# Modulation sums moved from VectorE to ScalarE (scaling) and GpSimd (adding) in a three-layer forward pass

## The chip, the cores and the metric

The kernel runs on one core of one Trainium2 chip. The metric is the device time of one execution in microseconds (us). The engines are TensorE (PE, with its weight loads as PEld), VectorE (DVE), ScalarE (ACT), GpSimd (POOL) and SyncE (SP, which only issues transfers here). Each engine takes its instructions in the order of the program and waits on semaphores for the others.

## The reference

One token sequence of 256 positions and 2048 features goes through three layers: a hybrid of gated linear attention and sparse attention with a feed-forward part, an attention layer with context tokens (`ev`), and a pooling layer (`od`). Everything is fp32. What the change touches is the modulation of the second and third layer, a vector times matrix product per layer:

```python
def _modulation(cvec, w, b):
    m = jax.nn.silu(cvec) @ w + b          # w: 2048 x 6144
    m = m[..., None, :]
    return m[..., :D_MODEL], m[..., D_MODEL:2 * D_MODEL], m[..., 2 * D_MODEL:]

# attention layer: for the tokens and for the context
shift, scale, gate = _modulation(c, mod_w, mod_b)
shift_c, scale_c, gate_c = _modulation(c_ctx, mod_w, mod_b)
h = _rmsnorm(x, pre_g) * (1 + scale) + shift
# pooling layer: for the tokens alone
shift, scale, gate = _modulation(c, mod_w, mod_b)
```

The rest is matrix products of 256 tokens with weights of 2048 or more rows, norms, and attention.

## The kernel before

The main work is a stream of 305 steps. A step makes one tile of 128 output features for 256 tokens: it takes two halves of 1024 x 128 weights (`w_main`, 512 KB each). Each half lands in one of four buffers `raw`; ScalarE copies it to `w_hi` in the rounded type fp32r (L776, function `hi`), VectorE subtracts to get the rest `w_lo` (L1002, function `lo`), and TensorE multiplies three products per 128x128 block: hi x hi, hi x lo, lo x hi (L411 to L413). That is 48 matmuls in a step, two PSUM banks in turn. The steps are grouped in stages (`STAGES`): conv, rest, out, up0, down0, up1, down1, up2, down2, ev_kv, ev_q, ev_z, ev_out, od_u, pool, od_z, od_out. In down2 a step has 36 matmuls; in out, down2, ev_out and od_out TensorE adds one matmul a step for a sum of squares, whose square ScalarE makes (L785).

Beside the main stream runs a side stream. Twelve of the stages (`MOD_GROUPS`) carry, in their first 16 steps, one group of modulation weights: 16 side tiles of 128 rows x 1024 columns (`w_side`, 512 KB), one a step, in two buffers `side`. VectorE multiplies the tile by the 128 values of silu(c) that belong to its rows and adds it to the running sum `mod_sum` (L1014, function `add_mod`). In four stages (`BOTH`: groups 0 to 3, which are rest, out, up0 and down0) it does so a second time from the same tile for the context vector, into the second half of `mod_sum`. When the sixteenth tile is in, TensorE sums `mod_sum` over the partitions with 128x1 matmuls at the end of the stage (L468, function `sum_mods`), VectorE reads them (L1038) and clears `mod_sum` (L1019).

The order of the work is written out by hand: each engine has its own program, with loops of two steps (`steps`). In step k of a stage
- SP (`loads`) issues the two raw loads of step k+2, each when `w_lo` of the half two steps before is done (`lo_ready`), and then side tile k, when tile k-2 has been added (`mods_added`);
- ScalarE (`ahead`) makes `w_hi` of step k+1, when the raw halves have landed and TensorE has used the same buffers for step k-1 (`halves_used`), and then what the stage asks for: a Silu (L754 in the up stages, L763 in the z stages, L838 in rest) or a square (L785);
- VectorE (`reading`) makes `w_lo` of step k+1, then the mod sum of tile k, then waits for TensorE to finish step k and reads its result out of PSUM (in conv with four taps, L1124 and L1127; in the up and z stages with a gate and a split, L1402 to L1408).

Of the kernel before, what the change touches and what calls it, by code (L numbers as in the profile page):

```python
# [25 lines left out]
ACT = mybir.ActivationFunctionType  # L26
# [119 lines left out]
def build(nc, x, ctx_in, w_main, w_side, cols_in, cons_in, gla_masks_in, counts_in, gate_w2_in, cmp_w2_in, out):  # L146
    stack = ExitStack()
    with stack:
# [3 lines left out]
        def S(name):  # L152
            if name not in sems:
                sems[name] = stack.enter_context(nc.semaphore(name))
            return sems[name]
# [135 lines left out]
        lo_ready = S("lo_ready")  # L291
        halves_used = S("halves_used")
        mods_added = S("mods_added")
        mods_summed = S("mods_summed")
        cmp_used = S("cmp_used")
        dve_read = S("dve_read")
# [105 lines left out]
        def _(pe):  # L402
# [58 lines left out]
            def sum_mods(stage):  # L461

                g = MOD_STAGES.index(stage)
                pe.wait_ge(mods_added, DT * (g + 1))
                vecs = 2 if MOD_GROUPS[stage] in BOTH else 1
                for t in range(8):
                    for c in range(vecs):
                        mm = pe.matmul(ps[:, 7, vecs * t + c:vecs * t + c + 1], mod_sum[:, c, t * P:(t + 1) * P],  # L468
                                       ones[:, 0:1], start=True, stop=True)
                mm.then_inc(mods_summed, 1)  # L470
# [275 lines left out]
        def gate_silu_steps(act, stage, silus):  # L746

            def extra(i, k):
                if k % 2:
                    return  # L750
                s = FIRST[stage] + k
                act.wait_ge(halves_used, i * 4 + (2 * s + 2))
                act.wait_ge(S("gate_y"), i + (silus + 1))
                act.activation(sg[:, 0, :], ps[:, s % 2, 0:T], ACT.Silu).then_inc(silu_ready, 1)  # L754
            return extra

# [11 lines left out]
        def _(act):  # L768
            def hi(i, s):

                for c in range(2):
                    slot = 2 * (s % 2) + c
                    act.wait_ge(raw_full[slot], i * 16 + 16 * (s // 2 + 1))
                    if s >= 2:
                        act.wait_ge(halves_used, i * 4 + (2 * s + c - 3))
                    act.activation(w_hi[:, slot, :], raw[:, slot, :], ACT.Copy).then_inc(hi_ready, 1)  # L776

            def ahead(stage, first=0, extra=None, squared=None, of=None):

                base = dve_reads(stage)  # L780

                def square(i, k):
                    act.wait_ge(dve_read, i * 2 + (base + k + 1))
                    src = of[:, k:k + 1, :] if isinstance(i, int) else of[:, bass.ds(i * 2 + k, 1), :]
                    act.activation(sq_tile[:, k % 2:k % 2 + 1, :], src, ACT.Square).then_inc(S(f"{squared}_sq"), 1)  # L785

                def body(i, k):
                    if FIRST[stage] + k + 1 < STEPS:
                        hi(i, FIRST[stage] + k + 1)
                    if extra is not None:  # L790
                        extra(i, k)
                    if squared is not None and k:
                        square(i, k - 1)
                if squared is not None:
                    first = 2
                steps(act, stage, body, first=first, last=2 if stage == "od_out" else 0)
                if squared is not None:
                    square(0, COUNT[stage] - 1)

# [6 lines left out]
            def root(name, buf):  # L806
                act.wait_ge(S(f"{name}_rs"), 1)
                act.activation(buf, buf, ACT.Sqrt).then_inc(S(f"{name}_rs"), 1)
# [10 lines left out]
            def from_psum(name, dst):  # L819
# [8 lines left out]
            hi(0, 0)  # L828
            act.activation(csil[:, :, :], col("cvec", 0, 32).rearrange("p (t c) -> p t c", c=2), ACT.Silu)\
               .then_inc(S("csil"), 1)  # L830
            root("attn", rstd[:, :])
            shift_hi("attn", sq, a_hi, None)
            ahead("conv", first=2)

            def conv_silu(i, k):

                if k % 2 == 0 and k < 28:
                    act.activation(pr[:, bass.ds(i, 1), :], pr[:, bass.ds(i, 1), :], ACT.Silu)  # L838
            act.wait_ge(dve_read, 16)
            ahead("rest", extra=conv_silu)  # L840
            act.activation(pr[:, 14:16, :], pr[:, 14:16, :], ACT.Silu).then_inc(S("g_silu"), 1)
# [150 lines left out]
                act.activation(o_tok[:, 0, g * 512:(g + 1) * 512], ps[:, g, :], ACT.Copy).then_inc(S("o_tok0"), 1)  # L992


        @block.vector
        def _(dve):
            def lo(i, s):
# [6 lines left out]

            def add_mod(stage, i, k):

                n, m = mod_half(stage, k)
                vecs = 2 if MOD_GROUPS[stage] in BOTH else 1
                dve.wait_ge(side_full[n % 2], i * 16 + 16 * (n // 2 + 1))
                if k or not isinstance(i, int):  # L1010
                    dve.wait_ge(mods_added, i * 2 + m)
                for c in range(vecs):
                    value = csil[:, k:k + 1, c] if isinstance(i, int) else csil[:, bass.ds(i * 2 + k, 1), c]
                    ins = dve.scalar_tensor_tensor(out=mod_sum[:, c, :], in0=side[:, n % 2, :], scalar=value,  # L1014
                                                   in1=mod_sum[:, c, :], op0=ALU.mult, op1=ALU.add)
                ins.then_inc(mods_added, 1)

            def clear_mods(g):
                dve.memset(mod_sum[:, :, :], 0.0).then_inc(S("mods_clear"), 1)  # L1019
# [632 lines left out]
```

## Time and profile before

| | |
|---|---|
| median of 3 runs | 2452.38 us (2448.59 to 2456.3) |
| span of the profiled execution | 2443.0 us |
| its own time against that median | 9.4 us lie around the span |
| TensorE busy, mean granted clock | 2199.2 us (90%), 0.920 |
| VectorE busy | 1576.2 us (65%) |
| ScalarE busy | 995.4 us (41%) |
| GpSimd busy | 0.2 us (4 small memsets) |
| transfers | 433.76 MB, mean 178 GB/s |

The profile gives the span, from the first to the last instruction, of one execution; the time of that execution outside the span is not recorded, so the difference to the median stands for it. Busy shares are averages over stages with different limits. The stages stand in the trace at these times: conv 42 to 149 us, rest to 323, the attention work of the first layer to 549, out to 657, up0 687 to 870, down0 to 974, up1 to 1161, down1 to 1255, up2 to 1395, down2 to 1488, ev_kv 1534 to 1616, ev_q to 1711, attention to 1872, ev_z to 1957, ev_out to 2059, and then the stages of the pooling layer, which carry no side tiles.

### The profile page before, as it was taken

The numbers are of one execution on the slowest core, as the hardware profiler recorded it, in microseconds if no ns is written. First come the engines' busy times: TensorE is split into PE (matmuls) and PEld (weight loads), VectorE is DVE, ScalarE is ACT, GpSimd is POOL, SyncE is SP. The second block draws the span as 40 slices with busy tenths as digits, with TensorE's granted clock in tenths as the row PEclk, the third lists the DMA queues.
The fourth block names the chain that finished last, engine by engine and source line by source line (L and its number), as shares of the span: only waits on it lengthen the run. The fifth ranks groups of instructions, "written<-read, shape, count | busy, mean of one in ns | idle before, by whom it ended". The sixth has DMA issues, their size and how long they took to land.

```text
span 2443.0 us, 45011 instructions
## 1 busy us (share of the span) xinstructions
PE 2199.2 (90%) x16718; PEld 2127.6 (87%) x16718; DVE 1576.2 (65%) x2077; ACT 995.4 (41%) x1230; POOL 0.2 (0%) x4
## 2 busy tenths in 40 slices
PE   5999987489799999999999996999689998888997
PEld 5999986369799999999999985999378998888997
DVE  5888564548787577764767576346656766666544
ACT  4346631333355632343333344223245633424642
POOL 0000000000000000000000000000000000000000
PEclk8999966569899999999999997999699998998998
DMA  4767521007567586765878682357003875444552
GB/s 174 245 239 270 184 80 44 0 1 241 172 220 236 174 287 227 263 226 186 269 259 273 200 294 85 100 181 273 6 1 127 271 248 171 138 138 142 185 181 95
DMA packets 119530, 433.76 MB, mean 178 GB/s; under 512 B 13216, under 2 KB 13600, under 8 KB 119216
## 3 DMA queue, kind: packets, MB, share of 16 engines
q1 hardware_dynamic: 119472, 432.98, 53.2%
q8 instruction: 37, 0.61, 0.1%
q14 instruction: 21, 0.17, 0.0%
HBM read 430.83 MB, written 2.10 MB: 177 GB/s over the span
## 4 chain that ended last, share of the span: by engine, by line
PE 69%; DVE 16%; DMA 8%; issue 4%; ACT 2%; SPq 1%; DVEq 1%; ACTq 0%
PE ps L411 19%; PE ps L413 19%; PE ps L412 19%; DMA side<-w_side 8%; DVE w_lo L1002 3%; PE ps L643 2%; PE ps L473 2%; PE ps L468 1%; DVE sq L1064 1%; PE ps L480 1%; DVE mod_sum L1014 1%; DVE at_max L1339 1%; PE ps L512 1%; PE ps L437 1%; PE ps L632 1%
## 5 line engine op out<-in xcount | busy, mean ns | idle before, releaser
L411 PE MATMUL ps<-a_hi,w_hi 128*128 128x256 f32 x3280 | 939.8, 287 | 58.4 <-DVE w_lo L1002 33.4
L412 PE MATMUL ps<-a_lo,w_hi 128*128 128x256 f32 x3280 | 934.2, 285 | 0.0
L413 PE MATMUL ps<-a_hi,w_lo 128*128 128x256 f32 x3280 | 933.8, 285 | 0.0
L776 ACT ACTIVATE w_hi<-raw 128x1024 fp32r<-128x1024 f32 x610 | 634.2, 1056 | 699.3 <-PE ps L413 636.0
L1002 DVE TENSOR_TENSOR w_lo<-raw,w_hi 128x1024 fp32r<-128x1024 f32 x610 | 718.8, 1220 | 108.3 <-ACT w_hi L776 105.6
L411 PEld LDWEIGHTS ps<-a_hi,w_hi 128*128 128x128 f32 x3280 | 635.8, 194 | 66.1 <-DVE w_lo L1002 35.5
L412 PEld LDWEIGHTS ps<-a_lo,w_hi 128*128 128x128 f32 x3280 | 636.0, 194 | 0.0
L413 PEld LDWEIGHTS ps<-a_hi,w_lo 128*128 128x128 f32 x3280 | 635.8, 194 | 0.0
L411 PE MATMUL ps<-b_hi,w_hi 128*128 128x256 f32 x1664 | 485.0, 291 | 17.6 <-DVE w_lo L1002 8.4
L413 PE MATMUL ps<-b_hi,w_lo 128*128 128x256 f32 x1664 | 473.8, 285 | 0.0
L412 PE MATMUL ps<-b_lo,w_hi 128*128 128x256 f32 x1664 | 473.7, 285 | 0.0
L1014 DVE SCALAR_TENSOR_TENSOR mod_sum<-side,csil,mod_sum 128x1024 f32<-128x1024 f32 x256 | 323.0, 1282 | 153.8 <-DMA side<-w_side 153.4
L411 PEld LDWEIGHTS ps<-b_hi,w_hi 128*128 128x128 f32 x1664 | 322.4, 194 | 24.2 <-issue 10.5
L412 PEld LDWEIGHTS ps<-b_lo,w_hi 128*128 128x128 f32 x1664 | 322.4, 194 | 1.2
L413 PEld LDWEIGHTS ps<-b_hi,w_lo 128*128 128x128 f32 x1664 | 322.2, 194 | 0.0
L1137 DVE COPY pr<-ps 128x256 f32 (+1 forms) x93 | 39.4, 424 | 171.4 <-PE ps L413 171.4
L754 ACT ACTIVATE sg<-ps 128x256 f32<-128x256 f32 x44 | 16.9, 385 | 146.8 <-PE ps L413 146.7
L632 PE MATMUL ps<-pr 128*128 128x256 f32 (+1 forms) x192 | 52.7, 422 | 18.0 <-DVE pr L1462 6.3
L776 ACT ACT_TABLE_LOAD x46 | 59.0, 1283 | 17.4 <-DVE pr L1127 11.3
L632 PEld LDWEIGHTS ps<-pr 128*128 128x128 f32 x192 | 37.4, 221 | 32.8 <-DVE pr L1462 7.2
L1371 DVE COPY pr<-ps 128x128 f32<-128x128 f32 x48 | 14.0, 292 | 62.5 <-PE ps L643 32.7
L473 PE MATMUL ps<-cons,prob 128*128 128x128 f32 x176 | 34.1, 327 | 20.5 <-DVE prob L1366 12.8
(242 smaller groups left out, 1462.6 us busy)
## 6 DMA issues: line engine op xcount, KB each, us to landing
raw<-w_main SPq DMA_DIRECT2D x610, 512.0 KB, 4.3
side<-w_side SPq DMA_DIRECT2D x200, 512.0 KB, 5.6
x_tok<-x_in SPq DMA_DIRECT2D x4, 512.0 KB, 6.0
ctx_tok<-ctx_tok SPq DMA_DIRECT2D x1, 2048.0 KB, 9.2
y_out<-o_tok SPq DMA_DIRECT2D x4, 512.0 KB, 2.7
cons<-cons_in SPq DMA_DIRECT2D x1, 542.0 KB, 8.0
table<-counts_tab SPq DMA_DIRECT2D x1, 512.0 KB, 10.1
table<-masks_in SPq DMA_DIRECT2D x1, 448.0 KB, 11.1
```

The source lines that it names most:

```text
L411: pe.matmul(out_ap, wh, act_hi[:, kt, :], start=first and n == 0, stop=False)
L412: pe.matmul(out_ap, wh, act_lo[:, kt, :], start=False, stop=False)
L413: mm = pe.matmul(out_ap, wl, act_hi[:, kt, :], start=False, stop=last and n == len(blocks) - 1)
L437: return pe.matmul(ps[:, 2, 0:T], ones, sq_tile[:, k % 2, :], start=k == 0, stop=k == COUNT[stage] - 1)
L468: mm = pe.matmul(ps[:, 7, vecs * t + c:vecs * t + c + 1], mod_sum[:, c, t * P:(t + 1) * P], ones[:, 0:1], start=True, stop=True)
L473: return pe.transpose(ps[0:ncols, bank, at_col:at_col + rows], src_ap, ident[base:base + rows, base:base + rows])
L632: mm = pe.matmul(ps[:, 2 + h % 3, part * T:part * T + a["keys"]], pr[:, a["q"](h), a["cols"]], pr[:, a["k"](h, part), 0:a["keys"]], start= ...
L643: mm = pe.matmul(ps[:, 5 + h % 2, 0:P], a["v"](h, part, b), a["prob_t"][:, h % 2, n, :], start=n == 0, stop=a["kind"] != "n" and n == len( ...
L776: act.activation(w_hi[:, slot, :], raw[:, slot, :], ACT.Copy).then_inc(hi_ready, 1)
L1002: dve.tensor_tensor(w_lo[:, slot, :], raw[:, slot, :], w_hi[:, slot, :].bitcast(F32), ALU.subtract)\
L1014: ins = dve.scalar_tensor_tensor(out=mod_sum[:, c, :], in0=side[:, n % 2, :], scalar=value, in1=mod_sum[:, c, :], op0=ALU.mult, op1=ALU.add)
L1137: dve.tensor_copy(tile(dst, i, k + k0), psum_tile(bank)).then_inc(dve_read, 1)
```

## The change

The running sum for the token vector leaves VectorE. ScalarE multiplies the side tile in place by the silu(c) values of its rows (`scale_mod`, a Copy with a scale that is a pointer to 128 values), and GpSimd, which had no program, adds the scaled tile to `mod_sum` (`add`). A side buffer is free when GpSimd has added it. In the four stages of `BOTH`, VectorE still makes the sum for the context vector from the unscaled tile, and ScalarE may overwrite the tile only after that (`mods_ctx`). ScalarE's loops are now cut after 16 steps in the stages with side tiles, and two indices are adapted to that.

```diff
@@ TensorE, sum_mods
                 pe.wait_ge(mods_added, DT * (g + 1))
+                pe.wait_ge(mods_ctx, DT * sum(MOD_GROUPS[name] in BOTH for name in MOD_STAGES[:g + 1])) \
+                    if any(MOD_GROUPS[name] in BOTH for name in MOD_STAGES[:g + 1]) else None
@@ ScalarE, gate_silu_steps
-                act.wait_ge(S("gate_y"), i + (silus + 1))
+                act.wait_ge(S("gate_y"), i + (silus + k // 2 + 1))
@@ ScalarE, ahead
+                def scale_mod(i, k):
+                    n, m = mod_half(stage, k)
+                    act.wait_ge(side_full[n % 2], i * 16 + 16 * (n // 2 + 1))
+                    if MOD_GROUPS[stage] in BOTH:
+                        g = MOD_STAGES.index(stage)
+                        both = DT * sum(MOD_GROUPS[name] in BOTH for name in MOD_STAGES[:g]) + k
+                        act.wait_ge(mods_ctx, i * 2 + (both + 1))
+                    value = csil[:, k:k + 1, 0] if isinstance(i, int) else csil[:, bass.ds(i * 2 + k, 1), 0]
+                    act.activation(side[:, n % 2, :], side[:, n % 2, :], ACT.Copy, scale=value).then_inc(mods_scaled, 1)
+
                 def body(i, k):
                     if FIRST[stage] + k + 1 < STEPS:
                         hi(i, FIRST[stage] + k + 1)
+                    if stage in MOD_GROUPS and k < DT:
+                        scale_mod(i, k)
                     if extra is not None:
                         extra(i, k)
...
-                steps(act, stage, body, first=first, last=2 if stage == "od_out" else 0)
+                steps(act, stage, body, first=first, last=2 if stage == "od_out" else 0,
+                      splits=[DT] if stage in MOD_GROUPS else ())
@@ GpSimd, a program of its own
+        @block.gpsimd
+        def _(pool):
+            def add(i, m, k):
+                n = m + (2 * CMP_HALVES if m >= CMP_AT else 0)
+                pool.wait_ge(mods_scaled, i * 2 + (m + 1))
+                if m or not isinstance(i, int):
+                    pool.wait_ge(mods_added, i * 2 + m)
+                pool.tensor_tensor(mod_sum[:, 0, :], side[:, n % 2, :], mod_sum[:, 0, :], ALU.add).then_inc(mods_added, 1)
+
+            for g in range(len(MOD_STAGES)):
+                pool.wait_ge(S("mods_clear"), g + 1)
+                add(0, DT * g, 0)
+                add(0, DT * g + 1, 1)
+                with pool.Fori(0, DT // 2 - 1) as i:
+                    add(i, DT * g + 2, 2)
+                    add(i, DT * g + 3, 3)
@@ VectorE, add_mod
+                if MOD_GROUPS[stage] not in BOTH:
+                    return
                 n, m = mod_half(stage, k)
-                vecs = 2 if MOD_GROUPS[stage] in BOTH else 1
+                g = MOD_STAGES.index(stage)
+                both = DT * sum(MOD_GROUPS[name] in BOTH for name in MOD_STAGES[:g]) + k
                 dve.wait_ge(side_full[n % 2], i * 16 + 16 * (n // 2 + 1))
-                if k or not isinstance(i, int):
-                    dve.wait_ge(mods_added, i * 2 + m)
-                for c in range(vecs):
-                    value = csil[:, k:k + 1, c] if isinstance(i, int) else csil[:, bass.ds(i * 2 + k, 1), c]
-                    ins = dve.scalar_tensor_tensor(out=mod_sum[:, c, :], in0=side[:, n % 2, :], scalar=value,
-                                                   in1=mod_sum[:, c, :], op0=ALU.mult, op1=ALU.add)
-                ins.then_inc(mods_added, 1)
+                if both or not isinstance(i, int):
+                    dve.wait_ge(mods_ctx, i * 2 + both)
+                value = csil[:, k:k + 1, 1] if isinstance(i, int) else csil[:, bass.ds(i * 2 + k, 1), 1]
+                dve.scalar_tensor_tensor(out=mod_sum[:, 1, :], in0=side[:, n % 2, :], scalar=value,
+                                         in1=mod_sum[:, 1, :], op0=ALU.mult, op1=ALU.add).then_inc(mods_ctx, 1)
```

Where it moves instructions can be seen in the loops of two steps. On ScalarE, the loop of stage up0 (steps 0 to 15 of it now, all 32 before) stood so before:

```order
L775 ISA [waits raw_full0]
L776 ACT_TABLE_LOAD
L776 ACTIVATE w_hi<-raw 128x1024 [waits halves_used]
L775 REGISTER_ALU [waits raw_full1]
L776 ACTIVATE w_hi<-raw 128x1024 [waits halves_used]
L753 REGISTER_ALU [waits halves_used]
L754 ACT_TABLE_LOAD
L754 ACTIVATE sg<-ps 128x256 [waits gate_y]
L775 REGISTER_ALU [waits raw_full2]
L776 ACTIVATE w_hi<-raw 128x1024 [waits halves_used]
L776 ACTIVATE w_hi<-raw 128x1024 [waits halves_used,raw_full3]
```

and stands so now (all but the register rows; L780 is the old L776, L758 the old L754):

```order
L780 ACT_TABLE_LOAD
L780 ACTIVATE w_hi<-raw 128x1024 [waits halves_used]
L780 ACTIVATE w_hi<-raw 128x1024 [waits halves_used]
L797 ISA [waits side_full0]
L799 ISA [waits mods_ctx]
L799 ACTIVATE side<-side,csil 128x1024
L758 ACT_TABLE_LOAD
L758 ACTIVATE sg<-ps 128x256 [waits gate_y]
L780 ACTIVATE w_hi<-raw 128x1024 [waits halves_used]
L780 ACTIVATE w_hi<-raw 128x1024 [waits halves_used,raw_full3]
L799 ISA [waits mods_ctx]
L799 ACTIVATE side<-side,csil 128x1024
```

A scaling with its waits for the side tile and for VectorE's context sum has come in behind each pair of `w_hi`; the two table loads stay.

On VectorE, one step in the loop of stage down0 (both vectors) stood so before:

```order
L1011 ISA [waits side_full0]
L1014 ISA [waits mods_added]
L1014 SCALAR_TENSOR_TENSOR mod_sum<-side,csil,mod_sum 128x1024
L1014 ISA
L1014 SCALAR_TENSOR_TENSOR mod_sum<-side,csil,mod_sum 128x1024
L1389 ISA [waits halves_used]
L1389 TENSOR_TENSOR res<-ps,res 128x256
L1002 TENSOR_TENSOR w_lo<-raw,w_hi 128x1024 [waits hi_ready]
L1002 TENSOR_TENSOR w_lo<-raw,w_hi 128x1024 [waits hi_ready]
```

and stands so now (L1038 is the old L1002, L1426 the old L1389):

```order
L1050 ISA [waits side_full0]
L1052 ISA [waits mods_ctx]
L1052 SCALAR_TENSOR_TENSOR mod_sum<-side,csil,mod_sum 128x1024
L1426 ISA [waits halves_used]
L1426 TENSOR_TENSOR res<-ps,res 128x256
L1038 TENSOR_TENSOR w_lo<-raw,w_hi 128x1024 [waits hi_ready]
L1038 TENSOR_TENSOR w_lo<-raw,w_hi 128x1024 [waits hi_ready]
L1050 REGISTER_ALU [waits side_full1]
```

One of two sums is gone, and the next sum stands behind the next two `w_lo` as before. GpSimd's loop is two adds with a wait for the scaling and for the add before.

## Rows read from the trace of the kernel before

**Rows 1.** The page's head and part 1: busy us (share) xinstructions.

```profile
span 2443.0 us, 45011 instructions
PE 2199.2 (90%) x16718; PEld 2127.6 (87%) x16718; DVE 1576.2 (65%) x2077; ACT 995.4 (41%) x1230; POOL 0.2 (0%) x4
```

**Rows 2.** Busy us by window: conv, rest, out, up0, down0, up1, down1, down2, ev_z, ev_out.

```profile
core 0: us, PE busy (x) PEld busy (x) DVE busy (x) ACT busy (x) POOL busy (x), PEclk, DMA share, GB/s
42.00:149.00 107.00, 99.57 (x782) 97.18 (x782) 88.25 (x115) 32.85 (x31) 0.00 (x0) 0.96 0.74 250
149.00:245.00 96.00, 96.00 (x782) 96.00 (x783) 82.80 (x81) 60.31 (x60) 0.00 (x0) 0.97 0.75 255
549.00:651.00 102.00, 100.95 (x800) 99.75 (x801) 83.39 (x81) 37.26 (x47) 0.00 (x0) 0.98 0.75 245
687.00:780.00 93.00, 87.19 (x716) 85.91 (x715) 77.59 (x84) 50.05 (x51) 0.00 (x0) 1.00 0.74 244
872.00:967.00 95.00, 92.50 (x761) 92.29 (x760) 81.99 (x81) 33.92 (x32) 0.00 (x0) 0.99 0.80 268
975.00:1160.00 185.00, 185.00 (x1539) 185.00 (x1537) 113.38 (x128) 70.07 (x80) 0.00 (x0) 1.00 0.67 222
1163.00:1254.00 91.00, 91.00 (x762) 91.00 (x760) 63.93 (x65) 33.62 (x32) 0.00 (x0) 1.00 0.81 270
1397.00:1485.00 88.00, 79.61 (x595) 73.36 (x594) 62.43 (x65) 38.92 (x47) 0.00 (x0) 0.98 0.84 280
1872.00:1954.00 82.00, 79.87 (x666) 79.58 (x664) 65.39 (x86) 51.90 (x58) 0.00 (x0) 1.00 0.82 272
1958.00:2058.00 100.00, 99.25 (x797) 98.02 (x796) 64.33 (x65) 38.20 (x47) 0.00 (x0) 0.99 0.73 247
```

**Rows 3.** Waits: engine line waited for: total us, times, longest.

```profile
DVE mod_sum L1014 <- DMA side<-w_side: 153.4, 145, 3.4
```

**Rows 4.** The chain that ended last, in conv: start us, us, what.

```profile
105.97 6.07 DMA side<-w_side
```

**Rows 5.** Timeline of VectorE in conv, from one late side tile on.

```profile
99.24 1.28 DVE L1014 SCALAR_TENSOR_TENSOR mod_sum<-side,csil,mod_sum 128x1024 f32<-128x1024 f32 x1 [0.99 <-DMA side<-w_side]
100.44 0.48 DVE L1124 TENSOR_SCALAR pr<-ps,cols 128x256 f32 x1
...
102.82 2.35 DVE L1002 TENSOR_TENSOR w_lo<-raw,w_hi 128x1024 fp32r<-128x1024 f32 x2
...
112.29 1.29 DVE L1014 SCALAR_TENSOR_TENSOR mod_sum<-side,csil,mod_sum 128x1024 f32<-128x1024 f32 x1 [1.18 <-DMA side<-w_side]
```

**Rows 6.** Part 5, costliest groups: xcount | busy us, mean ns | idle before.

```profile
L776 ACT ACTIVATE w_hi<-raw 128x1024 fp32r<-128x1024 f32 x610 | 634.2, 1056 | 699.3 <-PE ps L413 636.0
L1002 DVE TENSOR_TENSOR w_lo<-raw,w_hi 128x1024 fp32r<-128x1024 f32 x610 | 718.8, 1220 | 108.3 <-ACT w_hi L776 105.6
L1014 DVE SCALAR_TENSOR_TENSOR mod_sum<-side,csil,mod_sum 128x1024 f32<-128x1024 f32 x256 | 323.0, 1282 | 153.8 <-DMA side<-w_side 153.4
L754 ACT ACTIVATE sg<-ps 128x256 f32<-128x256 f32 x44 | 16.9, 385 | 146.8 <-PE ps L413 146.7
L776 ACT ACT_TABLE_LOAD x46 | 59.0, 1283 | 17.4 <-DVE pr L1127 11.3
```

**Rows 7.** The chain in the first attention: reciprocal over 1024, tensor-tensor over 2048 elements.

```profile
420.78 6.56 DVE g_rs L1249
...
430.63 2.30 DVE g_y L1258
```

**Rows 8.** The chain in down2: a landing.

```profile
1420.98 5.17 DMA side<-w_side
```

**Rows 9.** Timeline of TensorE at the ends of conv, down0 and ev_z.

```profile
145.37 0.80 PE L468 MATMUL ps<-cons,mod_sum 128*128 128x1 f32 x3 [3.39 <-DVE mod_sum L1014]
...
966.34 0.81 PE L468 MATMUL ps<-cons,mod_sum 128*128 128x1 f32 x4 [2.50 <-DVE mod_sum L1014]
...
1954.00 0.72 PE L468 MATMUL ps<-cons,mod_sum 128*128 128x1 f32 x5 [2.13 <-DVE mod_sum L1014]
```

More of the change, by code:

```diff
@@ L293, in build @@
         mods_added = S("mods_added")
+        mods_ctx = S("mods_ctx")
+        mods_scaled = S("mods_scaled")
         mods_summed = S("mods_summed")
@@ L830, in _ @@
                .then_inc(S("csil"), 1)
+            act.wait_ge(S("csil"), 1)
             root("attn", rstd[:, :])
@@ L837, in conv_silu @@
                 if k % 2 == 0 and k < 28:
-                    act.activation(pr[:, bass.ds(i, 1), :], pr[:, bass.ds(i, 1), :], ACT.Silu)
+                    at = bass.ds(i + k // 2, 1)
+                    act.activation(pr[:, at, :], pr[:, at, :], ACT.Silu)
             act.wait_ge(dve_read, 16)
```

## Prediction, before the result was known

> **What bounds the kernel now.** I read the page's busy shares first: TensorE is busy 90% of the span, VectorE 65%, ScalarE 41%, GpSimd not at all [rows 1]. VectorE is thus not a bound by its total, and taking work off it pays only where TensorE waits for it. So the windows by stage come next [rows 2]. From the matmul counts a step (48 matmuls, 49 with the sum of squares, 36 in down2) takes 91/762 x 48 = 5.73 us where TensorE is the limit (down1, and 185/1539 x 48 = 5.77 in up1, whose pattern up2 and ev_q repeat). For two steps, the natural unit because `side` has two buffers: conv 107/782 x 96 = 13.1 us, rest 11.8, out 12.5 (a step has 49), up0 12.5, down0 12.0, down1 11.5, ev_z 11.8, ev_out 12.3 with its 49. Only conv, up0, down2, slightly down0 and ev_z run behind TensorE's pace; there the excess over 11.5 us is all that a relief of VectorE can return.
>
> The waits tell what it is: VectorE stood 153 us, 145 times, for side transfers [rows 3]. The chain shows the loop in conv [rows 4, 5]: transfer lands, mod sum (1.20 us to the next start), conv taps (2.38), two `w_lo` (2.36), 0.79 until SP has issued two raw loads and the next side load, 6.07 us until that has landed, 0.25 until the sum starts: 13.05 us for two steps. SP is in order, so the side load stands behind raw loads that wait for `lo_ready`. That is the loop the change rewires.
>
> **The change part by part.** Durations [rows 6]: `w_hi` 1.06, `w_lo` 1.22, one mod sum 1.28, ScalarE's table load 1.28, a small Silu over 256 elements 0.39, which I take for the square and the residual add of that size too (0.4).
>
> VectorE loses 192 of 256 mod sums (192 x 1.28 = 246 us busy). ScalarE gains 192 scalings of 1024 elements per partition; the trace has no scaling with a pointer, the nearest row is `w_hi`, same engine and shape, so 1.06 each, 204 us on an engine that was 59% idle. That total costs nothing by itself. GpSimd gains 192 adds of 128x1024. No row shows such an add: the cheapest end is VectorE's `w_lo`, same operation and shape, 1.22; the dear end is the slowest instruction over 1024 elements in the trace, the reciprocal at 6.56 us. The add is nearer the first; I take 2.30, the row of a VectorE tensor-tensor over twice the elements [rows 7], because an engine that the kernel never uses for arithmetic should not be counted as fast as VectorE. The Trainium skill (GPSIMD Engine Reference, Performance versus the Vector engine) measured 4497 ns for an add over 2048 fp32 elements; an estimate by halving is 2.25 us. No run here shows it yet, and the sum would be the same by it.
>
> What matters is the new order of waits. A scaling waits for the side transfer, and behind it in ScalarE's queue stands the `w_hi` of the next step but one, and so `w_lo`, the raw loads and the next side load.
>
> (a) Stages with one vector, adds not in the way. Loop for two steps: scale 1.06, two `w_hi` 2.12, second `w_lo` 1.22, issue 0.79, landing. Landings on the chain are 5.17 to 6.07 [rows 4, 8]; I take 5.5 where loads are evenly spaced, 6.3 with the start in conv. Conv: 11.5, under the 11.8 of its neighbour, so 1.3 x 8 = 11 us gained. down1, up1, up2, ev_q: 10.7 to 11.1 (0.39 for the Silu), under TensorE's 11.5: no change. down2, the one stage where transfers and not TensorE set the pace before and after: scale 1.06 + square 0.4 + 2.12 + 1.22 = 4.80 stand in the place of sum 1.28 + residual add 0.4 + two `w_lo` 2.36 = 4.04: +0.76 x 8 = 6. ev_z: 1.06 + table 1.28 + 0.39 + 2.12 + 1.22 + 0.79 + 5.5 = 12.4 against 11.8: +0.54 x 8 = 4.
>
> (b) Stages with both vectors (rest, out, up0, down0). VectorE's sum must read `side` before ScalarE overwrites it, and VectorE's next sum stands behind the `w_lo` of the next step. That closes a loop within one step: sum 1.28, scale 1.06, [table load and Silu], two `w_hi` 2.12, second `w_lo` 1.22, next sum. Down0 and out: 5.68 and 6.1 (square), just under their 6.0 and 6.25: 0. In rest and up0 each pair holds two table loads and one Silu (the order shows them): 2 x (1.28 + 1.06 + 1.28 + 2.12 + 1.22) + 0.39 = 14.3. Rest: 14.3 - 11.8 = 2.5 x 8 = +20. Up0: 14.3 - 12.5 = 1.8 x 8 = +15. Before, the table loads were covered because `w_hi` came 1.5 steps ahead of its use; behind the scaling this lead is gone.
>
> (c) Ends. TensorE's 128x1 matmuls need the last sum. It comes later by scale + add (+3.36), less the sum 1.28 it replaces, some 0.2 for a hand-over: 2.3. In conv, down0 and ev_z TensorE already waited there (3.39, 2.50, 2.13 [rows 9]): 7. In out, down1, down2, ev_q and ev_out the margin hides between 0 and all of it: I take 1 each, 5. In rest and the up stages the sum is ready long before. Together +12.
>
> (d) Whether the add and VectorE's instructions run side by side. The trace has no GpSimd work, so: cheap end 0, dear end that an add and an instruction of VectorE with two SBUF operands (`w_lo`, sum) exclude each other for the add's whole 2.30. The add starts with the first `w_hi` after the scaling, so `w_lo`, due 1.06 later, would wait till 2.30. Then in (b) the step is 1.28 + 1.06 + 2.30 + 1.22 + 1.22 = 7.08: down0 +1.09 x 16 = 17, out +0.83 x 16 = 13; rest and up0 nothing, since table load and `w_hi` last 2.34. In (a) the loop is 1.06 + 2.30 + 2.44 + 0.79 + 5.5 = 12.1: down1, up1, up2, ev_q +0.63 x 8 x 4 = 20; conv 5.80 in place of 5.94: -1 instead of -11; down2 5.80 - 4.04 = 1.76 x 8 = 14 instead of 6; ev_out under its 12.3: 0. I take the dear end: in loops without slack each overlap shows in full, and the two would contend for 2.30 + 2.44 of every 5.8 us. The Trainium skill (SBUF — State Buffer, Who interferes with whom) says that a VectorE instruction with two SBUF inputs and a GpSimd instruction that reads SBUF exclude each other, whoever comes second blocked for the whole instruction. It speaks against this change; no run here shows it yet. By it the sum is the dear one, without it the cheap one.
>
> Sum, dear end: 20 + 15 + 13 + 17 + 20 + 14 + 4 - 1 + 12 = +114 us. Cheap end: 20 + 15 + 6 + 4 - 11 + 12 = +46. The profiled span is 2443.0 [rows 1]; the median of the runs is 2452.4, so 9.4 us lie around it, and 2443 + 114 + 9.4 = 2567.
>
> **The rivals.**
> Side by side (the cheap end): GpSimd slows nobody. For it: nothing in the trace couples the two. Against it: nothing in the trace could. 2443 + 46 + 9 = 2498.
> GpSimd becomes the bound: an add of 6.56. SP may load `side` again only after the add; from 2.12 + 1.22 + 0.79 = 4.1 us on the add outlasts that path and decides. Two steps are then 1.06 + 6.56 + 0.79 + 5.5 = 13.9 (15.2 with both vectors): down1, up1, up2, ev_q, ev_z, ev_out +2.4, 2.4, 2.4, 2.4, 2.1, 1.6 x 8 = 106; rest, out, up0, down0 +3.4, 2.7, 2.7, 3.2 x 8 = 96; down2 and conv +36; ends +50: about 2740. Against it: 6.56 is a reciprocal's.
> Not slower: VectorE, free of the 153 us of waits, delivers `w_lo` early, and ScalarE's waits for the side transfer fall into the 636 us that `w_hi` waits for TensorE anyway [rows 6]. This decides if the loop of (b) stays under 5.73 us a step in rest and up0, i.e. if sum and scaling overlap the `w_hi` of another step. Then conv -11, up0 -1.0 x 8, down0 -0.5 x 8, ev_z -0.3 x 8: -25, or 2427; with the 12 of the ends 2440. Against it: ScalarE's queue is in order and the scaling stands in front.
>
> **Numbers.** Exclusion 0.50 (2567), side by side 0.28 (2498), not slower 0.11 (2427 to 2450), GpSimd the bound 0.07 (over 2650), else 0.04. What can be told from no change here is 0.3%, 7 us. The forecast's own range is 2530 to 2610 (landing 5.2 to 6.1 us: 40 pairs x 0.9); with side by side it reaches down to 2480, and up to 2640 for an add of 3 us. Faster 0.08, same 0.05, slower 0.87.
>
> **What would show it.** Rest and up0 at about 14.3 us for two steps, VectorE's `w_lo` waiting for ScalarE's `w_hi`, and `w_hi` ending waits on `side`: (b). Down0 and out at 7.1 a step, with long `w_lo` or `w_lo` starting when an add ends: exclusion; at 6.0 and 6.25 and `w_lo` still 1.22: side by side. Conv at 11.8: (a) without exclusion. Adds over 4 us with SP's side loads released by GpSimd: the third case. Rest and up0 still under 12.5 would prove (b) wrong.

## The result, and the profile after

The changed kernel takes 2582.96 us in the median of 4 runs (2579.88 to 2586.41), the kernel before 2454.34 us (2448.59 to 2464.99): 5.4% slower, ratio 1.0536 with a 95% interval of 1.05 to 1.0573. The forecast was 2567 us.

The page's head, part 1 and four groups of part 5 of the changed kernel, in the place of [rows 1, 6] (L1038 is `w_lo`, L780 `w_hi`, L799 the scaling, L1021 the add, L1052 the context sum):

```profile
span 2584.6 us, 45692 instructions
PE 2247.6 (87%) x16718; PEld 2157.3 (83%) x16718; DVE 1517.5 (59%) x1885; ACT 1147.8 (44%) x1394; POOL 464.5 (18%) x196
L1038 DVE TENSOR_TENSOR w_lo<-raw,w_hi 128x1024 fp32r<-128x1024 f32 x610 | 877.1, 1478 | 336.9 <-ACT w_hi L780 334.4
L1021 POOL TENSOR_TENSOR mod_sum<-side,mod_sum 128x1024 f32<-128x1024 f32 x192 | 464.3, 2418 | 1732.0 <-ACT side L799 1710.5
L799 ACT ACTIVATE side<-side,csil 128x1024 f32<-128x1024 f32 x192 | 221.0, 1151 | 578.7 <-DMA side<-w_side 351.9
L1052 DVE SCALAR_TENSOR_TENSOR mod_sum<-side,csil,mod_sum 128x1024 f32<-128x1024 f32 x64 | 81.6, 1275 | 0.0
```

VectorE made 192 instructions fewer, yet its busy time fell by only 59 us and not by 246. Most of the rest is in its 610 `w_lo`, untouched by the change, which went from 1220 to 1478 ns in the mean: 158 us. The 141 of them that ran beside an add of GpSimd took 2.34 us in the mean, the 455 that met no add 1.22. The add takes 2.42 us (taken: 2.30), the scaling 1.15 (taken: 1.06). The waits, in the place of [rows 3] (total us, times, longest):

```profile
ACT side L799 <- DMA side<-w_side: 351.9, 125, 7.4
DVE w_lo L1038 <- ACT w_hi L780: 334.4, 167, 5.2
ACT w_hi L780 <- PE ps L415: 287.0, 153, 6.9
ACT side L799 <- DVE mod_sum L1052: 226.9, 64, 8.6
PE ps L413 <- DVE w_lo L1038: 96.0, 65, 17.0
```

VectorE's wait for side transfers has become ScalarE's, and `w_lo` now waits 334 us for `w_hi` (106 before [rows 6]): ScalarE's copies come late because the scaling stands in front of them.

By stage: the time from one clear of `mod_sum` to the next (L1019, now L1056) read from both profiled executions; gains and losses in us.

| stretch ending with | before | after | difference | forecast, with its end |
|---|---|---|---|---|
| conv | 107.1 | 105.9 | -1.3 | +1.3 |
| rest | 173.3 | 195.1 | +21.8 | +20 |
| out (with the attention work of layer 1) | 334.4 | 361.9 | +27.5 | +14 |
| up0 | 213.4 | 229.7 | +16.3 | +15 |
| down0 | 103.0 | 125.5 | +22.5 | +19 |
| up1, up2 | 327.8 | 336.3 | +8.5 | +10 |
| down1 | 93.9 | 102.8 | +8.8 | +6 |
| down2 | 93.1 | 101.8 | +8.7 | +15 |
| ev_q (with norms, ev_kv) | 222.2 | 232.0 | +9.7 | +6 |
| ev_z (with attention) | 245.8 | 261.5 | +15.7 | +6 |
| the rest of the program (ev_out) | 486.5 | 490.1 | +3.6 | +1 |

VectorE, ScalarE and GpSimd in one step of down0 (start us, us, engine, line, operation, idle before and its releaser; three views, one below the other):

```profile
993.26 3.74 DVE L1038 TENSOR_TENSOR w_lo<-raw,w_hi 128x1024 fp32r<-128x1024 f32 x2 [1.95 <-ACT w_hi L780]
996.92 1.27 DVE L1052 SCALAR_TENSOR_TENSOR mod_sum<-side,csil,mod_sum 128x1024 f32<-128x1024 f32 x1
1000.47 3.80 DVE L1038 TENSOR_TENSOR w_lo<-raw,w_hi 128x1024 fp32r<-128x1024 f32 x2 [1.94 <-ACT w_hi L780]
...
998.34 1.15 ACT L799 ACTIVATE side<-side,csil 128x1024 f32<-128x1024 f32 x1 [4.16 <-DVE mod_sum L1052]
999.39 1.99 ACT L780 ACTIVATE w_hi<-raw 128x1024 fp32r<-128x1024 f32 x2
...
999.65 2.40 POOL L1021 TENSOR_TENSOR mod_sum<-side,mod_sum 128x1024 f32<-128x1024 f32 x1 [4.87 <-ACT side L799]
```

The loop within one step can be read off: sum from 996.92, scaling from 998.34, `w_hi` from 999.39, the add from 999.65 to 1002.05; the two `w_lo` begin at 1000.47 but take 3.80 us in place of 2.36, because the first ends about 1 us after the add does. From one such pair to the next it is 7.21 us (1000.47 - 993.26); the forecast was 7.08. In up0 the table load replaces the exclusion:

```profile
778.66 1.28 DVE L1052 SCALAR_TENSOR_TENSOR mod_sum<-side,csil,mod_sum 128x1024 f32<-128x1024 f32 x1
783.65 2.36 DVE L1038 TENSOR_TENSOR w_lo<-raw,w_hi 128x1024 fp32r<-128x1024 f32 x2 [2.39 <-ACT w_hi L780]
...
780.10 1.16 ACT L799 ACTIVATE side<-side,csil 128x1024 f32<-128x1024 f32 x1 [2.80 <-DVE mod_sum L1052]
781.27 1.28 ACT L780 ACT_TABLE_LOAD   x1
782.56 2.00 ACT L780 ACTIVATE w_hi<-raw 128x1024 fp32r<-128x1024 f32 x2
...
781.33 2.41 POOL L1021 TENSOR_TENSOR mod_sum<-side,mod_sum 128x1024 f32<-128x1024 f32 x1 [5.06 <-ACT side L799]
```

Here the add is over (783.74) just when `w_lo` starts, which stays at 2.36 for two. Two steps take 14.8 us against a forecast of 14.3 (783.65 - 768.86, where the pair two steps earlier starts).

### The profile page after: what moved, and what is told of

The parts are those of the page before. It is cut to its first block, busy times and chain, and to the rows that moved or that the text cites. A ratio compares the mean times of both kernels' runs of the same rounds, so it can differ in the third digit from the quotient of the medians.

```text
span 2584.6 us, 45692 instructions
## 1 busy us (share of the span) xinstructions
PE 2247.6 (87%) x16718; PEld 2157.3 (83%) x16718; DVE 1517.5 (59%) x1885; ACT 1147.8 (44%) x1394; POOL 464.5 (18%) x196
## 4 chain that ended last, share of the span: by engine, by line
PE 47%; DVE 18%; DMA 13%; issue 12%; ACT 7%; SPq 1%; POOL 1%; ACTq 1%; DVEq 1%; POOLq 0%
DMA side<-w_side 13%; PE ps L413 12%; PE ps L415 12%; PE ps L414 12%; DVE w_lo L1038 5%; ACT w_hi L780 3%; PE ps L647 2%; DVE mod_sum L1052 2%; PE ps L477 2%; PE ps L472 2%; POOL mod_sum L1021 1%; PE ps L484 1%; DVE sq L1101 1%; SPq L348 1%; PE ps L636 1%
## 5 line engine op out<-in xcount | busy, mean ns | idle before, releaser
L1038 DVE TENSOR_TENSOR w_lo<-raw,w_hi 128x1024 fp32r<-128x1024 f32 x610 | 877.1, 1478 | 336.9 <-ACT w_hi L780 334.4
L1021 POOL TENSOR_TENSOR mod_sum<-side,mod_sum 128x1024 f32<-128x1024 f32 x192 | 464.3, 2418 | 1732.0 <-ACT side L799 1710.5
L780 ACT ACTIVATE w_hi<-raw 128x1024 fp32r<-128x1024 f32 x610 | 618.9, 1049 | 300.5 <-PE ps L415 287.0
L413 PE MATMUL ps<-b_hi,w_hi 128*128 128x256 f32 x1664 | 490.2, 295 | 31.5 <-DVE w_lo L1038 22.9
L799 ACT ACTIVATE side<-side,csil 128x1024 f32<-128x1024 f32 x192 | 221.0, 1151 | 578.7 <-DMA side<-w_side 351.9
L1052 DVE SCALAR_TENSOR_TENSOR mod_sum<-side,csil,mod_sum 128x1024 f32<-128x1024 f32 x64 | 81.6, 1275 | 0.0
L1439 DVE TENSOR_TENSOR gated<-pr,sg 128x256 f32<-128x256 f32 x32 | 32.5, 1015 | 62.3 <-ACT sg L767 62.3
L472 PEld LDWEIGHTS ps<-cons,mod_sum 128*128 128x128 f32 x256 | 42.2, 259 | 31.9 <-POOL mod_sum L1021 31.8
L472 PE MATMUL ps<-cons,mod_sum 128*128 128x1 f32 x256 | 42.6, 298 | 30.0 <-POOL mod_sum L1021 30.0
L636 PE MATMUL ps<-pr 128*128 128x256 f32 (+1 forms) x192 | 54.9, 438 | 15.7 <-DVE pr L1499 5.4
## 6 DMA issues: line engine op xcount, KB each, us to landing
table<-masks_in SPq DMA_DIRECT2D x1, 448.0 KB, 11.2
```

Of the source, the lines that this page charges most:

```text
L413: pe.matmul(out_ap, wh, act_hi[:, kt, :], start=first and n == 0, stop=False)
L636: mm = pe.matmul(ps[:, 2 + h % 3, part * T:part * T + a["keys"]], pr[:, a["q"](h), a["cols"]], pr[:, a["k"](h, part), 0:a["keys"]], start= ...
L799: act.activation(side[:, n % 2, :], side[:, n % 2, :], ACT.Copy, scale=value).then_inc(mods_scaled, 1)
L1021: pool.tensor_tensor(mod_sum[:, 0, :], side[:, n % 2, :], mod_sum[:, 0, :], ALU.add).then_inc(mods_added, 1)
L1038: dve.tensor_tensor(w_lo[:, slot, :], raw[:, slot, :], w_hi[:, slot, :].bitcast(F32), ALU.subtract)\
L1052: dve.scalar_tensor_tensor(out=mod_sum[:, 1, :], in0=side[:, n % 2, :], scalar=value, in1=mod_sum[:, 1, :], op0=ALU.mult, op1=ALU.add).the ...
```

## Experiments

All runs of a kernel stand beside runs of the kernel before on the same chip; the ratio is to those, with its 95% interval.

The forecast's word exclusion means here that an add of GpSimd and an instruction of VectorE with two SBUF operands can't run at the same time.

**Take the add's time away.** GpSimd adds 8 of 1024 columns.

```diff
-pool.tensor_tensor(mod_sum[:, 0, :], side[:, n % 2, :], mod_sum[:, 0, :], ALU.add).then_inc(mods_added, 1)
+pool.tensor_tensor(mod_sum[:, 0, 0:8], side[:, n % 2, 0:8], mod_sum[:, 0, 0:8], ALU.add).then_inc(mods_added, 1)
```

> The changed kernel with GpSimd adding 8 of the 1024 columns: the order and all hand-overs stay, the add's time goes (the sums of the other columns are left out). Theory 1 (exclusion: the add keeps VectorE's two-operand instructions waiting for its whole 2.4 us): back to the cheap end, about 2454 + 50 = 2504 us (2490 to 2520), w_lo at 1.22 instead of 1.48 us mean, down0 6.0 and out 6.25 us a step. Theory 2 (no exclusion, the price is in the hand-overs between three engines): only the ends get shorter by the add, 8 x 2.1 = 17 us, so about 2565, and down0 stays above 7 us a step.

Measured: 2506.55 us, ratio 1.0204 (1.0173 to 1.0235). `w_lo` is back at 1221 ns:

```profile
L1038 DVE TENSOR_TENSOR w_lo<-raw,w_hi 128x1024 fp32r<-128x1024 f32 x610 | 719.4, 1221 | 299.6 <-ACT w_hi L780 296.5 <-DVE mod_sum L1056 1.9 <-DVE pr L1560 0.2
```

down0 takes 109.8 us (125.5), down1 93.9 (as before the change), conv 98.8 (107.1 before: the relief of VectorE is real, and the only one). rest (194.3) and up0 (227.9) stay long. Theory 1 holds, at the forecast's cheap end of 2498 (+46) to within 9 us: the new order costs 50 us, and the other 1016 columns of the adds 76 more, part of which could be GpSimd's time alone; the next run looks at that. Two stages are dearer than the cheap end had them: down0 is 6.8 us above its time before the change where the sum had 2.3, and ev_z (256.7) is 10.9 above where it had 6.3.

**Keep GpSimd busy without reading.** The 8 columns, and then two fills.

```diff
+                pool.tensor_tensor(mod_sum[:, 0, 0:8], side[:, n % 2, 0:8], mod_sum[:, 0, 0:8], ALU.add)
+                pool.memset(mod_sum[:, 0, 8:HALF], 0.0)
+                pool.memset(spare[:, :], 0.0).then_inc(mods_added, 1)
```

> The changed kernel with GpSimd adding 8 columns and then filling 1016 + 512 columns with zeros (the sums are left out): GpSimd stays busy, an estimated 1.5 to 2.5 us per tile, but reads almost nothing. If VectorE waits only for GpSimd's reads: w_lo 1.22, time as in the run with 8 columns plus the ends, 2505 to 2525 us. If VectorE waits for whatever GpSimd does in SBUF: w_lo above 1.4 us mean and 2550 to 2585 us.

Measured: 2519.02 us, ratio 1.0259 (1.0223 to 1.0296). Its groups:

```profile
L1023 POOL MEMSET mod_sum<- 128x1016 f32 x192 | 181.6, 946 | 0.0
L1024 POOL MEMSET spare<- 128x512 f32 x192 | 100.9, 526 | 0.0
L1022 POOL TENSOR_TENSOR mod_sum<-side,mod_sum 128x8 f32<-128x8 f32 x192 | 44.4, 231 | 1819.1 <-ACT side L800 1805.2 <-DVE mod_sum L1059 13.9
L1041 DVE TENSOR_TENSOR w_lo<-raw,w_hi 128x1024 fp32r<-128x1024 f32 x610 | 719.4, 1221 | 299.0 <-ACT w_hi L781 295.9 <-DVE mod_sum L1059 1.9 <-DVE pr L1563 0.2
```

And its timeline in down0, GpSimd and VectorE:

```profile
987.19 0.20 POOL L1022 TENSOR_TENSOR mod_sum<-side,mod_sum 128x8 f32<-128x8 f32 x1 [4.87 <-ACT side L800]
987.33 0.94 POOL L1023 MEMSET mod_sum<- 128x1016 f32 x1
988.22 0.52 POOL L1024 MEMSET spare<- 128x512 f32 x1
...
988.09 2.36 DVE L1041 TENSOR_TENSOR w_lo<-raw,w_hi 128x1024 fp32r<-128x1024 f32 x2 [1.95 <-ACT w_hi L781]
```

The fills overlap the first `w_lo` (988.09 to 988.74) and it isn't stretched. Only 0.65 us overlap here, less than the add's, but in the whole trace 54 `w_lo` ran beside fills for 0.5 us or more, and all of them took 1.21 to 1.23 us. So VectorE's two-operand instruction waits for the add and not for the fill. The Trainium skill (SBUF — State Buffer, Who interferes with whom) says that a VectorE instruction with two SBUF inputs contends with a GpSimd instruction that reads SBUF and not with one that only writes it; this run and the one with full adds agree with it. By these runs alone it could be something else in which an add differs from a fill.

The fills did hold another instruction, the cast from SBUF to SBUF in the up and z stages, first VectorE and then GpSimd:

```profile
2002.15 0.29 DVE L1446 CAST b_hi<-gated 128x256 f32 x1
2005.76 1.06 DVE L1446 CAST b_hi<-gated 128x256 f32 x1 [0.15 <-DVE gated L1442]
...
2005.27 0.94 POOL L1023 MEMSET mod_sum<- 128x1016 f32 x1
2006.15 0.52 POOL L1024 MEMSET spare<- 128x512 f32 x1
```

The first cast meets no fill, the second ends 0.15 us after the second fill; 10 of the 76 casts took 0.77 to 1.45 us.

With this run the change can be split. The spans of the profiled executions, less the attention work of the first layer (whose length varies from kernel to kernel, see below), grow by 55 us from the kernel before to the 8-column adds, by 4 from there to the fills, and by 71 from the fills to the full adds. GpSimd's time as such is thus cheap (though the fills keep it busy for 1.7 us per tile, not 2.4), and the hold on VectorE is the dear part.

**The exclusion alone, in the old order.** The kernel before with an add per side tile on GpSimd that nobody waits for; it starts when VectorE's sum of that tile is done, and writes bf16.

```diff
+                pool.wait_ge(mods_added, i * 2 + (m + 1))
...
+                pool.tensor_tensor(spare[:, :], cons[:, 0:1024], cons[:, 128:1152], ALU.add).then_inc(spared, 1)
```

> The kernel before with one GpSimd add of 128x1024 per side tile beside it, started by each mod sum; it reads constants and writes a spare tile, and nobody waits for it. Exclusion: the next two w_lo wait for the add's end, 2.4 us after the sum instead of 0.4: +2 us in each loop of two steps that has no slack. With 1.28 + 2.4 + 2.36 + 0.79 + 5.8 = 12.6 against 11.5: +9 in down1, up1, up2, ev_q, ev_z each, +16 in down2, +14, 8, 8, 12 in rest, out, up0, down0, 0 in conv (its taps read PSUM): 2454 + 105, so 2540 to 2570 us, w_lo 1.4 to 1.6 us mean. No exclusion: 2454 and w_lo 1.22.

Measured: 2607.64 us, ratio 1.0647 (1.0622 to 1.0672), `w_lo` 1617 ns. The exclusion alone costs more than the whole change did, and 38 to 68 us more than I had reckoned (2540 to 2570). It is not the changed kernel's exclusion to the letter: here each add starts just when the next `w_lo` may. Its timeline in up1 shows two things that I left out, VectorE first, GpSimd below:

```profile
1111.05 4.56 DVE L1021 TENSOR_TENSOR w_lo<-raw,w_hi 128x1024 fp32r<-128x1024 f32 x2
1118.16 2.15 DVE L1425 CAST b_hi<-gated 128x256 f32 x1
...
1111.29 3.24 POOL L1004 TENSOR_TENSOR spare<-cons 128x1024 bf16<-128x1024 f32 x1 [4.48 <-DVE mod_sum L1033]
1117.77 2.39 POOL L1004 TENSOR_TENSOR spare<-cons 128x1024 bf16<-128x1024 f32 x1 [3.24 <-DVE mod_sum L1033]
```

An add that comes in while `w_lo` runs takes 3.24 us: it waits too, so whoever comes second waits. And the small cast of 256 columns, with one SBUF operand, took 2.15 us; the 39 of its 76 executions that met an add took 1.2 us or more, the other 37 0.30: not only two-operand instructions are held. up1 and up2 (201.8 and 154.2 us; 187.8 and 140.0 before), where that cast stands in the loop, lost 14 us each for the 9 I gave them. That is the smaller part of the miss: out itself lost 15 us (8 reckoned), up0 16 (8), down0 19 (12) and rest 19 (14), and 9 us lie in the attention work of the first layer, where no add runs. down2 lost 12.8 for 16.

**Undo one part.** The four stages with both vectors as before, the other eight changed (ScalarE's scaling and the adds skipped for `BOTH`, both sums on VectorE).

```diff
-                    if stage in MOD_GROUPS and k < DT:
+                    if stage in MOD_GROUPS and MOD_GROUPS[stage] not in BOTH and k < DT:
                         scale_mod(i, k)
...
+            alone = [g for g in range(len(MOD_STAGES)) if MOD_GROUPS[MOD_STAGES[g]] not in BOTH]
+            for j, g in enumerate(alone):
...
+                for c in range(2):
+                    value = csil[:, k:k + 1, c] if isinstance(i, int) else csil[:, bass.ds(i * 2 + k, 1), c]
```

> The change in the eight stages with one vector only; rest, out, up0 and down0 have both sums on VectorE again, as before. By the intervals between the clears of mod_sum, rest gained 22, out 27 (with the attention work), up0 16 and down0 22 us through the change: 87 in all. If each stage pays for its own order, the time is 2583 - 87 = 2496 us (2488 to 2506). If the price lies in the transfers or in GpSimd over the whole program, it stays above 2520.

Measured: 2528.5 us, ratio 1.0301 (1.0266 to 1.0336), so 32 us over what was expected. rest, up0 and down0 came back to 173.0, 216.1 and 105.7, and out itself to its 112.1 before the change. Two things had been reckoned wrongly. Part of the 27 us of the stretch that ends with out is not out's: 9 us of it are in the attention work here too (below). And the stages with one vector were longer than in the changed kernel's profile (down1 106.0 against 102.8, up2 148.9 against 144.4), 14 us together. That called for the control:

> The changed kernel as it is, beside the next three kernels on one chip: 2583 us within 0.3%, as before. If transfers land later here than in its first profile (side 5.6 us instead of 5.2 to 5.3 in down1 and down2), the stages with one vector take about 3 us more each, as they did in the run with both sums back on VectorE, and the time comes to about 2595; if not, that run's extra has another cause.

Measured: the changed kernel again, 2591.91 us, ratio 1.0573 (1.055 to 1.0597), with side transfers landing in 5.7 us in down1 (5.2 in its first profile), and down1 105.0, up2 148.1. That fits a landing in series with the loop, which no slack absorbs, in down1 and the up stages; ev_z (260.3) and down2 (101.7) did not grow. By the ratios the part undone is worth 58 us against the changed kernel's first runs and 67 against these. What is left, 72 us (2528.5 - 2456.1, the kernel before beside it), is not all the eight other stages': in the profile, 83 us longer than that of the kernel before, 9 are in the attention work and 5 in up0 and down0.

**Table loads.** A small Silu ahead of the loops of rest, up0 and ev_z keeps the table in place, so that the loads in the loops go.

```diff
+            act.activation(at_coef[:, :], col("attn_g", 0, 16), ACT.Silu)
             ahead("rest", extra=conv_silu)
...
-            act.activation(sg[:, 1, 0:2], ident[:, 0:2], ACT.Copy).then_inc(silu_ready, 1)
+            act.activation(sg[:, 1, 0:2], ident[:, 0:2], ACT.Silu).then_inc(silu_ready, 1)
...
+            act.activation(at_sink[:, :], col("sink", 0, 8), ACT.Silu)
             ahead("ev_z", extra=z_silu_steps(act, "ev_z", 0))
```

> The changed kernel with a small Silu ahead of the loops of rest, up0 and ev_z, so that no table is loaded inside them (one load of 1.28 us a step gone in 48 steps). Theory 2 (a serial loop without exclusion): rest and up0 lose 1.28 us a step, 41 us together, ev_z some 8 more: about 2535. Theory 1 (exclusion): behind the scaling w_lo now has to wait for the end of the add, 2.4 us, as in down0, so the step falls from 7.45 only to 7.2 us: 2583 - 8 - 2 = 2573 us (2560 to 2580), and w_lo in rest and up0 goes from 1.22 to about 1.8 us mean.

Measured: 2596.45 us, ratio 1.0557 (1.051 to 1.0604), against ratio 1.0573 of the control: nothing gained, where 10 us were expected. rest and up0 go from 195.1 and 229.5 only to 192.6 and 228.3, ev_z not at all (263.2 for 260.3); `w_lo` rises to 1534 ns. What the table load leaves, the add takes. With the 8-column adds as well:

> The run with 8-column adds (the other sums are left out) plus the small Silu ahead of the loops, so neither exclusion nor table loads. If step (b) is right in its parts, sum 1.28 + scale 1.15 + two w_hi 2.0 + w_lo 1.22 is 5.7 us, under TensorE's pace: rest goes from 194 back to 174, up0 from 228 to 214, ev_z 5 to 8 less: 2506 - 41 = 2465 us (2455 to 2475). If the table loads are not what makes rest and up0 long, it stays at 2506.

Measured: 2468.57 us, ratio 1.0079 (1.0047 to 1.011). rest 179.2, up0 215.0, the stretch with ev_z 246.0 (256.7 without the Silu). So without exclusion the table loads in rest, up0 and ev_z cost 38 us; with it, taking them out gives nothing. Each of the two, exclusion and table load, hides the other.

**SP's order.** The loop through the side transfer was what the change had hoped to shorten; it can be shortened at its longest part. SP issues side tile k in front of the raw loads of step k+2.

```diff
                     for c in range(count):
-                        for half in range(2):
-                            load(i, 2 * (s0 + k + c) + 4 + half)
                         if mods:
                             n, m = mod_half(stage, k0 + k + c)
                             side_load(i, n, None if m in (0, 1, CMP_AT, CMP_AT + 1) else (mods_added, i * 2 + (m - 1)))
+                        for half in range(2):
+                            load(i, 2 * (s0 + k + c) + 4 + half)
```

> The kernel before with SP issuing side tile k in front of the two raw loads of step k+2 instead of behind them: the tile no longer waits for w_lo and two issues, and lands about one w_lo pair earlier. Theory (the loop of two steps through the side transfer bounds conv, up0, down0, down2, ev_z): conv 107 to 97, up0 -7, down0 -3, down2 -5, ev_z -2: 2454 - 27 = 2427 us (2418 to 2438). Rival (the transfers' total is the bound there, 1.5 MB a step): no change, since the raw halves land as much later as the side tile lands earlier.

Measured, on the kernel before: 2422.69 us, ratio 0.987 (0.9842 to 0.9898), 1.3% faster than the kernel before, with the whole interval below 1. conv 97.2 (107.1), up0 207.5 (213.4), down0 98.7 (103.0), down2 78.5 (93.1): three times what I gave down2. The rival, that the transfers' total is the bound there, is ruled out. ev_z, to which I gave 2 us, did not gain (248.5, 245.8 before). On the changed kernel:

> The changed kernel with the same exchange on SP. The loop through the side transfer gets slack, so the stages with one vector lose what they gained through exclusion (down1, up1, up2, ev_q, down2, ev_z: about 35 us together); the serial loop within a step in rest, out, up0, down0 (sum, scale, w_hi, w_lo) holds no transfer and stays. So 2583 - 35 = 2548 us (2535 to 2560), with rest and up0 still at 14.8 us for two steps. If the transfer is in the loop of those four stages as well, it falls below 2520.

Measured: 2515.86 us, ratio 1.0267 (1.0244 to 1.029), 32 us better than expected, and below the 2520 that was to say that the transfer is in the loop of those four stages as well. The stages say otherwise. down1, up1, up2, ev_q and ev_z are back at their times before the change (94.4, 187.7, 140.4, 222.6, 246.3), down2 is at 81.1 and conv at 101.5; rest 195.3, up0 229.5 and down0 125.6 haven't moved. The expectation had given the stages with one vector 35 us; against the control's profile they lost 78, down2 alone 21. The two kinds of loop are apart: the one of two steps holds the transfer, the one of one step does not.

> The kernel before with side tile k issued in front of the raw loads and without table loads in the loops of rest, up0 and ev_z. There w_hi is 1.5 steps ahead of its use, so the table loads are covered: the same as the run with the exchange alone, 2423 us (2415 to 2430). If they stood in the way in up0 or ev_z, up0 drops under 205 and it falls below 2412.

Measured: 2417.17 us, ratio 0.9841 (0.9814 to 0.9867): the lowest time, though its interval overlaps that of the exchange alone. rest (172.0) and up0 (208.8) stand where the exchange alone has them (172.3, 207.5), so the loads there were covered in the old order; ev_z takes 244.2 for 248.5.

## Why the prediction was right, and where it was off

The forecast's main line held: exclusion, given a chance of 0.50, came true in its mechanism and in size, 2567 us for 2582.96. The runs bear out both halves of the sum, the new order (+46 forecast, 50 measured with 8-column adds) and what the add does to VectorE (68 more forecast, 76 measured with full adds, the fills putting nearly all of it on the hold).

- What bounds the kernel: right for conv, up0, down0 and down2, the stages that a shorter side loop speeds up; without the full add conv fell to 98.8 us. For ev_z it was wrong: the shorter side loop gave nothing there.
- (b), the loop of one step: right in kind and size, rest +21.8 for 20, up0 +16.3 for 15, down0 +22.5 for 19. The scaling at 1.15 in place of 1.06 makes 1.4 us of it in each stage, the add at 2.42 in place of 2.30 another 1.9 in down0.
- (d), the exclusion: the dear end was right, and was shown by taking the reading away, and by adding it to the old order. It was the least certain term, 68 of the 114 us.
- down2 was over-reckoned (+15 for 8.7): transfers landed in 5.3 us there where 6.1 had been the median before (5.17 in [rows 8] was the quick end). The sum left the landing as it was; 0.8 us less in each of 8 loops is an estimated 6 us.
- ev_z was under-reckoned (+6 for 15.7), in two ways. Its order with the table load alone was dearer than (a) had it: with 8-column adds it took 256.7, 10.9 over the kernel before, and 246.0 when the table load went too. And I had the exclusion hold `w_lo` and sums only. With full adds and no table load it took 263.2, so the exclusion alone is enough to make it long. The gate of the z stages (L1439) also reads two SBUF operands. Of its 16 in ev_z 15 were held, every second one from near the add's start (2.3 us), the others for the add's tail (1.0 us):

```profile
2019.89 2.33 DVE L1439 TENSOR_TENSOR gated<-pr,sg 128x256 f32<-128x256 f32 x1 [0.46 <-ACT sg L767]
2032.86 2.41 POOL L1021 TENSOR_TENSOR mod_sum<-side,mod_sum 128x1024 f32<-128x1024 f32 x1 [3.56 <-ACT side L799]
2033.21 2.35 DVE L1439 TENSOR_TENSOR gated<-pr,sg 128x256 f32<-128x256 f32 x1 [0.35 <-ACT sg L767]
```

  In the pooling layer, where no add runs, its 16 instructions took 0.43 us. In the up stages its first operand lies in PSUM: all 44 took 0.41 to 0.43 us. In the changed kernel none of those met an add, but in the run with spare adds 24 did, and took the same.
- The stretch with out: +27.5 for 14, of which 11.2 lie in the attention work of the first layer (from the clear of `mod_sum` to the copy of the mixer's output 233.5 us, 222.3 before), where there is no side tile and no add; out itself is +16.4. Of two windows of the same work, the first of the changed kernel, the second of the kernel before, the granted clock is the column ahead of the last two:

```profile
500.00:540.00 40.00, 35.30 (x122) 27.71 (x123) 19.02 (x71) 14.60 (x57) 0.00 (x0) 0.52 0.00 1
```

```profile
480.00:520.00 40.00, 33.79 (x120) 25.15 (x120) 20.40 (x75) 17.10 (x65) 0.00 (x0) 0.62 0.00 1
```

  In both TensorE was busy for 34 to 35 of the 40 us. In the changed kernel it is granted its lower level, 1.2 GHz, for more of it (0.52 of the full clock in place of 0.62). This doesn't go with the change: the same work took 238.4 us in the fast kernel with SP's exchange, 221.7 in the slower one with 8-column adds, and 229 to 231.5 in the eight other profiles, of old and new order alike. What decides it from kernel to kernel stays open.
- The ends (c) were under-reckoned, +12 for 22. TensorE's waits for the last sum, before and after, over the whole kernel:

```profile
L468 PE MATMUL ps<-cons,mod_sum 128*128 128x1 f32 x256 | 38.1, 281 | 8.0 <-DVE mod_sum L1014 8.0
L472 PE MATMUL ps<-cons,mod_sum 128*128 128x1 f32 x256 | 42.6, 298 | 30.0 <-POOL mod_sum L1021 30.0
```

  conv (3.4 to 5.6) grew as forecast. down0 went from 2.5 to 7.3, and down1 and ev_q, to which I gave 1 us each, from nothing to 4.8. That is as much as those two stages took beyond the forecast (+8.8 and +9.7 for 6). With 8-column adds the total was 8.6.
- Outside the span: the 9.4 us were not that. The executions whose span and time are both known took some 1.8 us more than their span (2586.41 and 2584.6 for the changed kernel's profiled one). So the profiled execution of the kernel before was an estimated 7.6 us quicker than the median, and its attention work, at 222.3, one of the two shortest of the twelve profiles. As the forecast was to be compared with the median, the term did no harm.
- The sum: 114 us against 141.6 between the two profiled spans, and 128.6 between the medians. Of the 28 missing to the spans, 11 are the attention's clock and 9 are ev_z; in the rest, some 18 us that rest, out, up0, down0, down1, ev_q and ev_out took beyond their terms stand against 10 that conv, up1, up2 and down2 had too much. So the mechanism was right in most stages, but that the total came within 16 us of the median is in part luck.

## What to carry to other kernels

An engine that is 65% busy is no bound, and moving work off it can put a wait in front of other work: look at what is queued behind each new wait, and whether a copy that ran ahead of its use loses that lead. The GpSimd adds here (2.42 us, both operands in SBUF) held VectorE's two-operand instructions until they were over, so such an add belongs where VectorE has nothing of the kind to do. Where a loop runs through a transfer, first try to move the transfer's issue ahead in its queue: here two swapped statements gave 28 us (1.3%), more than the 25 that the most hopeful rival had the change win.

## What the hardware showed that was not expected

A GpSimd add of 128x1024 in fp32 takes 2.42 us beside this work, a fill of 128x1016 takes 0.95 us; ScalarE's copy with a pointer as scale takes 1.15 us, 0.1 more than the `w_hi` copy of the same size. The add held not only instructions with two SBUF operands but also a cast from SBUF to SBUF of 256 columns (0.3 to 2.15 us), and was itself held by a running `w_lo` (2.4 to 3.24 us). Fills, which left `w_lo` alone, held that cast too (up to 1.45 us). VectorE's instructions of 256 columns with an operand in PSUM kept their time beside adds. The landing of the same side transfers in down1 differed between two profiles of one kernel, 5.2 and 5.7 us.
